# A two-layer hybrid diffusion block with experts: a GpSimd drain dropped, scatter rows copied ahead, y tiles read whole, one modulation product moved

## What is computed

```python
for l in range(2):
    mod  = (silu(c)     @ w_ada[l] + b_ada[l]).reshape(6, D)     # modulation rows: shift, scale, gate, twice
    modc = (silu(c_ctx) @ w_ada[l] + b_ada[l]).reshape(6, D)
    h = modulate(rmsnorm(x, g_mix[l]), mod[0], mod[1])           # the same for ctx with modc
    q, k, v, ... = split(h @ w_in[l])
    heads = [differential attention, window attention with sinks, gated convolution]
    x = x + mod[2] * (concat(heads) @ w_out[l])
    h2 = modulate(rmsnorm(x, g_ffn[l]), mod[3], mod[4])
    y = grouped_moe(h2)            # 16 experts, the 2 best of one group of 4 for each token, weighted
    x = x + mod[5] * y
return rmsnorm(x, g_final)
```

## Time and profile before

| what | us |
|---|---|
| runs of the kernel before | 1211.78, 1214.02, 1206.96 |
| their median | 1211.78 |
| the profiled execution: its own time | 1216.56 |
| its span, from the first to the last instruction | 1214.8 |

### The profile page before, as it was taken

The page is one execution under the profiler, slowest core; times in us unless marked ns, Lnnn a source line. Parts: engine busy times, 40 slices in busy tenths (PEclk is TensorE's granted clock), DMA queues, the critical chain, the costliest instruction groups (busy, mean ns, idle before and its releaser), DMA issues. The chain is left out here.

```text
span 1214.8 us, 23396 instructions
## 1 busy us (share of the span) xinstructions
PE 971.6 (80%) x8536; PEld 529.7 (44%) x8537; DVE 464.1 (38%) x1008; ACT 257.1 (21%) x497; POOL 224.5 (18%) x364
## 2 busy tenths in 40 slices
PE   3899999999889399999989429998887397755880
PEld 1344444355446255555545225543554254322440
DVE  1159505555535433333323166606633422211233
ACT  2100112343312022222212020113511122111110
POOL 2100000121001124333433230000000123211331
PEclk9699999999987599999989869999988598877895
DMA  9966612995003668999999196115007299999983
GB/s 368 391 263 259 260 54 81 364 398 206 1 1 149 255 257 332 413 370 414 422 420 419 44 386 237 70 69 208 1 1 285 107 393 412 411 421 425 415 361 127
DMA packets 52747, 317.92 MB, mean 262 GB/s; under 512 B 6984, under 2 KB 7064, under 8 KB 30160
## 3 DMA queue, kind: packets, MB, share of 16 engines
q1 hardware_dynamic: 40144, 284.70, 58.3%
q0 software_dynamic: 9344, 20.54, 4.6%
q10 hardware_dynamic: 3200, 11.86, 2.6%
HBM read 309.13 MB, written 12.65 MB: 265 GB/s over the span
## 5 line engine op out<-in xcount | busy, mean ns | idle before, releaser
L1608 PE MATMUL ps<-ring,HT 128*128 128x512 f32 (+1 forms) x672 | 299.2, 598 | 8.1 <-DVEq L554 5.7
L1608 PE MATMUL ps<-ring,area 128*32 128x256 f32 x3936 | 248.9, 404 | 42.4 <-DMA ring<-in_w 30.1
L1608 PE MATMUL ps<-area 128*32 128x256 f32 (+5 forms) x1896 | 216.3, 390 | 25.6 <-DVE area L1516 11.5
L1608 PEld LDWEIGHTS ps<-ring,HT 128*128 128x128 f32 x672 | 127.1, 195 | 156.0 <-issue 148.9
L1608 PEld LDWEIGHTS ps<-ring,area 128*32 128x32 f32 x3936 | 133.3, 116 | 130.2 <-issue 48.7
L1608 PEld LDWEIGHTS ps<-area 128*32 128x32 f32 (+2 forms) x1896 | 119.7, 136 | 49.3 <-issue 15.4
L1534 DVE COPY area<-ps 128x256 f32<-128x256 f32 x65 | 27.6, 425 | 249.6 <-PE ps L1850 249.6
L1608 PE MATMUL ps<-HT,area 128*32 128x256 f32 x704 | 86.7, 402 | 25.0 <-DMA area<-in_w 21.5
L1063 ACT ACTIVATE area<-ps 64x256 f32<-64x256 f32 x63 | 23.8, 378 | 377.3 <-PE ps L1608 377.3
L830 POOL DMA_INDIRECT area<-h_rows,area x68 | 71.2, 1048 | 118.7 <-DVEq L554 62.7
L1063 ACT ACT_TABLE_LOAD x63 | 80.8, 1283 | 38.5 <-DVEq L1527 37.4
(11 more groups left out here) (197 smaller groups left out, 813.0 us busy)
## 6 DMA issues: line engine op xcount, KB each, us to landing
ring<-in_w SPq DMA_DIRECT2D x66, 2048.0 KB
ring<-in_w_ada SPq DMA_DIRECT2D x24, 2048.0 KB
ring<-in_w_in SPq DMA_DIRECT2D x10, 2048.0 KB
HT<-in_w SPq DMA_DIRECT2D x10, 2048.0 KB
area<-in_w SPq DMA_DIRECT2D x10, 2048.0 KB
area<-in_w SPq DMA_DIRECT2D x20, 1024.0 KB
ring<-in_w_out SPq DMA_DIRECT2D x4, 2048.0 KB
area<-expert_rows ACTq DMA_DIRECT2D x12, 512.0 KB, 6.6
```

Of the source, the lines that this page charges most:

```text
L1608: return t_.matmul(out, lhsT, rhs, start=first, stop=last_)
```

## The change

Four edits, three of them at the end of the expert stage.

- **No drain.** `barrier(pool, bar(l, 5))` becomes `pass_barrier(bar(l, 5))` in both layers.
- **Scatter rows early.** In `scatter` the copy of the row numbers and the wait for it stand ahead of the wait for `y_rdy`. Since `sidx` may now be overwritten while the scatter before it is in flight, the loop waits for that scatter first. The first pair of the loop is written out ahead of it.
- **y in one transfer a tile.** ACT reads each tile of `expert_rows` with one transfer of 1 MB in place of two of 512 KB.
- **One product moved.** Quad (1, 1), called `LATE`, leaves the fillers of layer 0's attention. Its four loads become the first of layer 1, three of them free to go as soon as their slots are, the fourth after the second y tile has landed (SP's wait at line 707 moves there). PE computes it between the fifth barrier of layer 0 and the transposes of layer 1, in PSUM bank 7, which the transposes leave out. DVE adds the bias at the end of stage 1, ahead of its barrier. POOL loads the bias right behind the fifth barrier of layer 0, and stores and awaits the rows in stage 2 of layer 1.

```diff
@@ bank_plan
+        if l == LATE[0]:
+            put(("ada",) + LATE, bank=7)
-            put(("nT", l, g))
+            put(("nT", l, g), range(8 if l == 0 else 7))
@@ front_units
-    out = [("ada", 0, j) for j in range(4)] if l == 0 else []
+    out = [("ada", 0, j) for j in range(4)] if l == 0 else [("ada",) + (LATE[0], 4 * LATE[1] + j) for j in range(4)]
@@ attention_steps
-    dense = ([("A", q) for q in range(QUADS)] if l == 0 else []) + ...
+    dense = ([("A", q) for q in range(QUADS) if q != LATE[1]] if l == 0 else []) + ...
@@ SP
+                    if l and name == ("ada", l, 4 * LATE[1] + 3):
+
+                        sp.wait_ge(y_in[1], 16 * l)
...
-                if l < DEPTH - 1:
-
-                    sp.wait_ge(y_in[1], 32 * (l + 1))
@@ POOL, stage 2 of layer 1
+                else:
+                    pool.wait_ge(mod_sb, MODS.index(LATE) + 1)
+                    store_mod(MODS.index(LATE))
+                    pool.wait_ge(mod_out[LATE], 64)
                 pass_barrier(bar(l, 2))
@@ POOL, experts
                 def scatter(m, r):
 
-                    hold(pool, y_rdy[l], m + 2, pool_passed)
+                    if not isinstance(m, int):
+                        hold(pool, scat[l][r], pool.snap(sent) * 8, pool_passed)
                     g.tensor_copy(sidx[r], TS[:, bass.ds(m, 1)]).then_inc(sidx_set[l], 1)
                     hold(pool, sidx_set[l], m + 1, pool_passed)
+                    hold(pool, y_rdy[l], m + 2, pool_passed)
                     pool.indirect_dma_start(y_rows, ...)
...
-                barrier(pool, bar(l, 5))
+                pass_barrier(bar(l, 5))
+                if l + 1 == LATE[0]:
+                    load_bias(MODS.index(LATE))
@@ ACT, combine
-                    for k in range(2):
-                        act.dma_start(Y[:, i, k], y_v[:, i, k]).then_inc(y_in[i], 16)
+                    act.dma_start(Y[:, i], y_v[:, i]).then_inc(y_in[i], 16)
@@ DVE, stage 1
+                if l == LATE[0]:
+                    mod_rows(LATE)
                 barrier(dve, bar(l, 1))
@@ PE, stage 1
+                if l == LATE[0]:
+                    ada(*LATE)
                 for q in range(8):
```

42 lines of the change are left out of this document (21 added, 21 removed).

## The result

The changed kernel takes 1200.27 us, median of 15 runs (1196.57 to 1205.10), against 1209.68 for the kernel before in the same comparison (15 runs, 1202.85 to 1215.26). The ratio is 0.993, with a 95% interval of 0.9915 to 0.9945: 6.6 to 10.3 us less, 8.5 in the middle. The forecast was 1195.9 in a range of 1187 to 1206. The time lies in the range and the sign is right, but about half of the forecast gain of 15.9 us came.

What follows compares the result with a forecast made beforehand. PE bounds layer 0's experts, the weight stream layer 1's, an unhidden scatter-to-combine chain the end. Drains -10.9, scatters -2.1, y 0, attention -3.8, and +0.3, +0.3, +0.1, +0.2 sum to -15.9: from 1211.78 to 1195.9 us, range 1187 to 1206.

Steps and rivals of the forecast that it cites:

- Drains, -10.9: Fifth barriers: dropping POOL's drain gains 6.75 us in layer 0 and 4.14 in layer 1; bounds 0 and -10.9.
- as long as whatever the drain waited for is needed by nobody else: Condition on the drain gain at the fifth barriers, 6.75 us in layer 0 and 4.14 in layer 1.
- Rival (a): Fifth barriers: the drain's wait is only handed on, so the change gains 5.0 us, giving 1206.8; chance 0.10.
- Scatter rows, -2.1: Last y copy to its scatter: copy and wait done beforehand save 1.07 us in layer 0, 1.06 in layer 1.
- the new wait holds nobody: Expert loop: POOL's wait for the scatter two blocks back, issued some 12 us before, costs nothing.
- y in one transfer, 0 within 0.5 a layer: Reads of y before the combine: one transfer a tile changes nothing, between -0.5 and +0.5 us a layer.
- Attention, -3.8: Layer 0's attention, units 6 to 8 without filler: 18.5 us instead of 22.3; bounds -1.5 and -7.1.
- Rival (d): Layer 0's attention onward: without filler TensorE's clock stays at 1.2 GHz, giving 1219.7 us; chance 0.03.
- Where the product arrives, +0.7 in all: Between the layers: last-quarter tie +0.3, bias addition on DVE +0.3, bias load beside the first y tile +0.1 us.
- the tie at the last quarter: Before layer 1's transposes: product's last quarter ends 21.6 us after ACT's issue, transposes could start at 21.57; +0.3, between 0 and +3.
- rival (b): Between the layers: the moved quad becomes the bound, holding the transposes back by 3 us, giving 1198.9; chance 0.11.
- Scatters in the loop, (c): Layer 0's expert loop: forecast took nothing; the rival has eight waits giving 1.07 us each, -8.6 more, 1187.3; chance 0.04.

Runs made afterwards that it cites:

- e1: Kernel before with only the GpSimd drain at the fifth barrier dropped in both layers (semaphore pass instead); ratio 0.9912.
- e2: Kernel before with only the scatter rows copied early and the first pair of scatters moved in front of the loop; ratio 1.0015.
- e4: Changed kernel with its other three edits undone, so only the modulation product is moved into the combine; ratio 0.9992 against the kernel before.
- e9: Kernel with only the product moved, plus its bias loads issued ahead of the wait for the last scatter's landing; ratio 1.0019 against the kernel before.
- e3: Kernel before with only y read in one transfer a tile instead of two; ratio 1.0009.
- e5: Changed kernel with a GpSimd drain put back in layer 0 behind its barrier and the four bias loads; 1194.43 us, ratio 0.9890 against the kernel before.
- e7: Changed kernel with two extra tiles of scatter rows and layer 0's drain put back ahead of the bias loads; ratio 0.9914 against the kernel before.
- e10: Changed kernel with layer 0's drain back, two extra scatter-row tiles, bias loads before the last scatter's landing, y in two transfers; 1198.95 us, ratio 0.9887.
- e8: Kernel before with one more GpSimd drain in each turn of the expert loop, the barrier's drain kept; 1239.93 us in its one run.
- e11: Kernel before with drains dropped, layer 0's put back behind its barrier, early scatter rows with two extra tiles, product not moved; 1201.8 us, ratio 0.9899.

## Why the prediction was right or wrong

The time of 1200.27 us lies in the range, and the sign is right. The gain does not follow the sum as well as that sounds: it is 8.5 to 9.4 us where the sum had 15.9, and the forecast of 1195.9 comes out as near as 4.4 us partly because it started from the 1211.78 us of three runs, 2.1 above the 1209.68 of fifteen, which is luck. The terms one by one:

**Drains, -10.9: the mis-sized step is "as long as whatever the drain waited for is needed by nobody else".** I had read the difference of 6.75 and 4.14 us as a sign that the drains measure something outstanding, and looked for who would need it: the reads, the bias load, the final gain. I did not look at the next drain. At the barriers it was visible: 0.68 us at 719.8 with no DMA since the last drain, 6.75 behind 82 indirect DMAs. The whole price is carried to the next drain of POOL (7.37 us in e1, which is 6.75 and the 0.6 behind the rsqrts). In layer 1 that one stands beside the output, in layer 0 between the transposes and the first projection, where 1.3 us show in e1. In the changed kernel it is 2.1 (3.61 against 1.50), since the drain bills the four bias loads too (7.70 against 7.37), the transposes are through sooner, and 0.2 to 0.3 of it is the bias addition. Measured alone: -8.6 by stages, -10.3 by the median, whose interval of -14.8 to -6.4 holds both. Rival (a), that the wait is handed on, was right as a mechanism and wrong in place and size: handed on to another barrier, and mostly covered there.

**Scatter rows, -2.1: measured +0.6 in layer 0 and -0.7 in layer 1.** Alone, in e2, it was -0.2 and -0.7. Two steps failed. Of the 1.57 us I let 0.50 stay, and 0.88 stay. And "the new wait holds nobody" was wrong at the one place that counts, the last two scatters of layer 0, which also stand behind the landing of an earlier scatter: e2 lost there most of what it had won, and in the changed kernel POOL waits 1.12 us for it, since three loads of the moved product keep the DMA engines busy until then (e4, where the wait was 2.01). I had priced these loads at nothing, as being in a time "in which DMA had little to carry". It had the scatters to carry.

**y in one transfer, 0 within 0.5 a layer:** +0.6 and +0.1. Just outside the bound in layer 0.

**Attention, -3.8:** -4.5 in the changed kernel (57.0 to 52.5) and -3.1 in e4; the kernels with the edit show 52.5 three times and 54.0 four times. The way to read it, from layer 1's stretch without filler, held. The stretch of rows 7 took 17.8 us against 22.3 in the changed kernel and 19.2 in e4, around the 18.5 of layer 1. The step between them is the 1.5 us of the prediction: the stretch ran at a clock of 1.00 in the changed kernel and at 0.91 in e4. The term was right on the mean of seven traces (-3.7), and the changed kernel's -4.5 is the lucky draw of it. Rival (d), that the clock would stay low behind it, fell. The rule that the Trainium skill has in "TensorE: Matmul & The Clock Gate", section "Part 1: The HAM clock gate", that the throttled clock is the default and activity lifts it, bears on this: with filler the clock was 1.00 in this stretch before, without it it fell in four traces of seven.

**Where the product arrives, +0.7 in all: this is the largest miss.** In e4 it is +4.3. "+0.1" for the bias load was 1.3 (0.6 to 0.7 in the changed kernel, where it meets the tile at another time), the scatters' hold 2.0 (1.1 in the changed kernel), and the tie at the last quarter came out 1.1 to 1.3 late. I had the bounds of 0 and +3 for that last one alone, and in the changed kernel its later transposes ran faster by as much (3.65 us from the first's start to the last's, not 4.96), so that rival (b) did not come true as a price. The error is one of kind: I counted bytes and their rate, and asked for each load whether it comes in time, but not which transfer on the critical path it shares the engines with. (The bias load costs its 1.3 only where it runs beside the second tile: in e9, where it runs ahead of the reads, that wait is gone.)

**Scatters in the loop, (c):** 264.6 us against 265.0, and 266.3 in e2 alone. Taking nothing was right; the tie in rows 13 was one.

**The sum.** By stages of the profiled pair: attention -4.5, B -2.8, C -4.2, together -11.5, where I had -15.9. The change's parts alone give -8.7 (e1), -0.6, +1.9 and +1.4 by the same stages, together -6.0. So the parts do not add. What the traces show of the 5.5 us between: attention ran at the full clock in the changed kernel and not in e4 (1.4); POOL's wait for the earlier scatter is 0.9 shorter, since with the early copy part of it passes beside the last y copy; DVE's wait for the second tile is 0.7 shorter; the late last quarter costs 0.3 and not 0.7 from the normalisation to the projection (9.92 against 9.58 in e1, 8.68 against 7.97 in e4 and before), since PE waits for POOL's handed-on drain anyway; and e3's trace has 1.1 in the last scatter and the transposes that its edit does not explain. Together 4.5. The median has -9.4, the ratio -8.5; the stages are one execution each, and no closer agreement is to be had from them.

## What to carry to other kernels

Before a drain is dropped, find the next one on the same engine: where it bills by what was issued since the last, the bill moves, and belongs in a stretch where that engine idles (e5: 7.70 to 0.67 us at the place that counts). Work that is moved into an idle stretch is priced by the transfers that it brings there, against those on the critical path (e4); taking one of them out of the way can let the next one meet the path (e7, e10). When repeated traces of unchanged code differ by more than the effect, cut them into the stages that the edit touches, look at the granted clock of each, and change one part at a time.

## What the runs showed of the hardware

- A drain of GpSimd takes longer by 0.08 us for each DMA, direct or indirect, that GpSimd has issued since its last drain, though all have landed: 0.22 us behind 2 (e8), 4.14 behind 50, 6.75 behind 82 (before). Behind the rsqrts of the combine 0.6 us come on top (0.68 behind none, 7.37 behind 82 in e1).
- With a scatter on its way it waits for it: the 30 drains in e8's loop took 2.8 to 9.2 us and ended 0.21 us (twice 0.37) after the scatter's landing.
- An indirect DMA of GpSimd starts 0.86 to 0.89 us after its release in most places, whether a copy or a semaphore of DVE releases it (1.21 in layer 1 of e7, e10 and e11); a second one right behind starts 0.30 us after the end of the first.
- DVE starts on the first tile of y in layer 0 5.7 to 5.9 us after the first read is issued with four transfers of 1 MB, and 5.1 to 5.5 us with eight of 512 KB; the smaller ones are better for a consumer that works tile by tile.
- With 256 KB of bias, read as rows repeated over partitions, beside the reads of y the total rate was 328 GB/s for some 4 us in e4 and 329 in the changed kernel (688 to 692), and 418 in e2 without them, with the DMA engines fully busy in all three.
- The fourth tile of y landed 18.6 us after the first read with a load in packets of 8192 bytes beside it (e10), and 13.2 us with one in packets of 2048 bytes (e11).
- The part of the kernel that no edit touched took 1076 to 1091 us over twelve traces, with clocks of 0.83 and 0.94 in the same 30 us of code; the stretch without filler in layer 0's attention ran at 1.00 in three traces and at about 0.91 in four, 17.8 and 19.2 us.
